# Three operations of the retention branch moved to later places in two engines' orders: the block transpose, the upper half and the remainder of the w_b product's input

## The reference

```python
h = rmsnorm(x, g_mix)
z = h @ w_in                                    # 1024 x 5888, nine parts
aq, ak, av, rq, rk, rv, rg, ga, gb = jnp.split(z, SPLIT_POINTS, axis=-1)
ya = sliding_window_sink_attention(aq, ak, av, sinks) @ w_a
r = chunkwise_retention(rq, rk, rv)             # 4 heads, 256 rows x 1024
r = r * lax.rsqrt(jnp.mean(r * r, axis=-1, keepdims=True) + EPS)
r = r.reshape(B, S, RET_V) * jax.nn.silu(rg.astype(jnp.float32))
yb = r.astype(x.dtype) @ w_b                    # its input is what the change moves
mixed = jax.nn.sigmoid(ga) * ya + jax.nn.sigmoid(gb) * yb
x = x + mixed @ w_out
```

## Time and profile before

| | us |
|---|---|
| median of 3 runs | 1009.88 (1009.08 to 1010.19) |
| the profiled execution's own time | 1010.19 |
| its span | 1008.4 |
| TensorE busy | 1000.7 (99%) |
| VectorE busy | 726.4 (72%) |
| ScalarE busy | 501.6 (50%) |
| mean granted TensorE clock | 0.999 |

### The profile page before, as it was taken

How to read it: one execution, slowest core, us unless ns; L and a number is a source line. 1 busy time by engine, 2 the same in 40 slices (tenths; PEclk the granted TensorE clock), 3 DMA queues, 4 the chain that set the end, 5 groups by cost and what they waited for, 6 DMA issues and landing times.

```text
span 1008.4 us, 13509 instructions
## 1 busy us (share of the span) xinstructions
PE 1000.7 (99%) x5621; PEld 846.4 (84%) x5621; DVE 726.4 (72%) x805; ACT 501.6 (50%) x610; POOL 170.6 (17%) x129
## 2 busy tenths in 40 slices
PE   9999999999999999999999999999999999999997
PEld 7888777888888888888877888888887899899796
DVE  5785785766566565785785767788877767789974
ACT  6544563454444545454564355344468555644352
POOL 0530000000000000430000020000000149169730
PEclk9999999999999999999999999999999999999999
DMA  9797564555655455596574567546544744355451
GB/s 336 238 300 255 180 196 167 174 185 183 205 173 207 167 179 176 188 296 232 180 231 152 165 169 266 188 170 213 202 167 139 247 168 168 125 168 148 115 188 42
DMA packets 106396, 192.80 MB, mean 191 GB/s; under 512 B 9352, under 2 KB 20704, under 8 KB 106208
## 3 DMA queue, kind: packets, MB, share of 16 engines
q1 hardware_dynamic: 106160, 191.85, 58.2%
q10 hardware_dynamic: 176, 0.09, 0.0%
HBM read 182.79 MB, written 6.82 MB: 188 GB/s over the span
## 4 chain that ended last, share of the span: by engine, by line
PE 98%; DMA 1%; DVE 0%; ACT 0%; SPq 0%; issue 0%; DVEq 0%; ACTq 0%
PE bank L816 13%; PE bank L819 12%; PE bank L818 12%; PE bank L1121 11%; PE bank L841 10%; PE bank L845 9%; PE bank L852 9%; PE bank L1125 6%; PE bank L1203 2%; PE bank L1430 1%; PE bank L998 1%; PE bank L1014 1%; PE bank L1417 1%; PE bank L843 1%; PE bank L850 1%; PE bank L1106 1%
## 5 line engine op out<-in xcount | busy, mean ns | idle before, releaser
L1911 DVE TENSOR_TENSOR w_lo<-arena,w_hi 128x2048 fp32r<-128x2048 f32 (+1 forms) x80 | 185.0, 2323 | 99.1 <-ACT w_hi L1518 98.8
L1911 DVE TENSOR_TENSOR w_lo<-raw,w_hi 128x2048 fp32r<-128x2048 f32 (+1 forms) x78 | 180.7, 2327 | 82.5 <-ACT w_hi L1518 82.4
L1518 ACT ACTIVATE w_hi<-raw 128x2048 fp32r<-128x2048 f32 (+1 forms) x83 | 157.1, 1893 | 106.4 <-PE bank L819 72.9
L1518 ACT ACTIVATE w_hi<-arena 128x2048 fp32r<-128x2048 f32 (+1 forms) x80 | 151.3, 1891 | 106.1 <-PE bank L819 82.3
L1121 PE MATMUL bank<-hT,w_hi 128*128 128x512 f32 x504 | 123.4, 391 | 0.0
L2539 POOL TENSOR_TENSOR rstd<-mean,const 128x1 f32<-128x1 f32 (+1 forms) x16 | 9.1, 578 | 633.8 <-DVE mean L1920 464.7
L1121 PEld LDWEIGHTS bank<-hT,w_hi 128*128 128x128 f32 x504 | 92.2, 188 | 17.5
L816 PE MATMUL bank<-w_hi,hT 128*128 128x512 f32 (+1 forms) x248 | 95.3, 384 | 0.0
L819 PE MATMUL bank<-w_hi,hT 128*128 128x512 f32 (+1 forms) x224 | 85.5, 382 | 0.0
L818 PE MATMUL bank<-w_lo,hT 128*128 128x512 f32 (+1 forms) x224 | 85.5, 382 | 0.0
L816 PE MATMUL bank<-w_hi,uT_hi 128*128 128x512 f32 x208 | 81.2, 390 | 0.0
(11 more groups left out here) (356 smaller groups left out, 1917.0 us busy)
## 6 DMA issues: line engine op xcount, KB each, us to landing
arena<-in_w_in SPq DMA_DIRECT2D x22, 1024.0 KB, 5.6
raw<-in_w_in SPq DMA_DIRECT2D x20, 1024.0 KB, 5.7
arena<-in_w_up SPq DMA_DIRECT2D x16, 1024.0 KB, 5.5
raw<-in_w_up SPq DMA_DIRECT2D x16, 1024.0 KB, 5.3
arena<-in_w_down SPq DMA_DIRECT2D x16, 1024.0 KB, 5.2
raw<-in_w_down SPq DMA_DIRECT2D x16, 1024.0 KB, 5.2
raw<-in_e_w_in SPq DMA_DIRECT2D x6, 1024.0 KB, 5.2
arena<-in_e_w_in SPq DMA_DIRECT2D x6, 1024.0 KB, 5.3
```

The lines of the kernel that those rows point to most:

```text
L1518: act.activation(w_hi[:, p % SPLIT_RING, :, 0:n], raw_at(p)[:, :, 0:n], copy).then_inc(hi_ready, 1)
L1911: dve.tensor_tensor(w_lo[:, s, :, 0:n], raw_at(p)[:, :, 0:n], w_hi[:, s, :, 0:n].bitcast(F32), ALU.subtract).then_inc(lo_ready, 1)
```

## The change

Three instructions change place, in each of the two layers:

- VectorE's block transpose into `r_rows` moves from the third softmax to the head of iteration 11, ahead of `w_lo` of piece 24.
- ScalarE's copy to `uT_hi` moves behind its share of window 10 (the exponentials of the fourth softmax), so that it stands ahead of `w_hi` of piece 25 and the evacuation of group 11.
- VectorE's subtraction to `uT_lo` moves from the fourth softmax to behind the loop over the groups: behind `w_lo` of piece 25 and ahead of its share of window 11.

```diff
@@ ScalarE
                 for g in range(W_IN_GROUPS):
                     if l or g:
                         step(p + 2 * g)
+                    window(l, g - 1)
                     if g == W_IN_GROUPS - 1:
                         act.wait_ge(r_turned, l + 1)
                         act.activation(uT_hi[:, :, :], r_rows, copy).then_inc(r_hi, 1)
-                    window(l, g - 1)
                     if g != RQ:
                         step(p + 2 * g + 1)
                     group_out(l, g)
@@ VectorE
-            def beside_exp(l, g):
-
-                if g == 7:
-                    retention_mean(l, 1)
-                if g == W_IN_GROUPS - 3:
-                    dve.wait_ge(h_blocks, 16 * BLOCKS * (l + 1))
-                    turn_blocks(r_rows, h_moved, KD).then_inc(r_turned, 1)
-                if g == W_IN_GROUPS - 2:
-                    dve.wait_ge(r_hi, l + 1)
-                    dve.tensor_tensor(uT_lo[:, :, :], r_rows, uT_hi[:, :, :].bitcast(F32), ALU.subtract).then_inc(r_lo, 1)
-
...
                 if SCORES_AT <= g < SCORES_AT + PAIRS:
-                    softmax(l, g - SCORES_AT, between=lambda: beside_exp(l, g))
+                    softmax(l, g - SCORES_AT, between=(lambda: retention_mean(l, 1)) if g == 7 else lambda: None)
...
                         turn_blocks(rT, r_moved, 2 * RET_HEADS).then_inc(rT_ready, 1)
+                    if g == W_IN_GROUPS - 1:
+                        dve.wait_ge(h_blocks, 16 * BLOCKS * (l + 1))
+                        turn_blocks(r_rows, h_moved, KD).then_inc(r_turned, 1)
                     if g != AKV and (l or g):
                         step(p + 2 * g)
...
+                dve.wait_ge(r_hi, l + 1)
+                dve.tensor_tensor(uT_lo[:, :, :], r_rows, uT_hi[:, :, :].bitcast(F32), ALU.subtract).then_inc(r_lo, 1)
                 window(l, W_IN_GROUPS - 1)
```

## The result

The changed kernel takes 1020.49 us (median of 4, 1019.94 to 1021.77) against 1009.62 us beside it (median of 4 runs of the kernel before): a ratio of 1.0107, 95% interval 1.0092 to 1.0124. It is 10.9 us slower, where 7.4 had been forecast as the likeliest and 1020.6 was the end of the range. Its profiled execution took 1020.46 us, with a span of 1018.7.

A forecast was written before the change was run, and what follows sets the result against it. TensorE was taken as the bound, busy 1000.7 of 1008.4 us. Two stalls of 3.65 us, 7.4 with wake-ups and nothing for the clock, added to the 1009.88 median gave 1017.3 us; range 1015.4 to 1020.6.

The forecast's parts named there:

- the stall: TensorE ahead of w_b's first matmul, waiting for uT_lo: 3.65 us a layer, 7.4 us for both with wake-ups.
- Hidden, with 0.3 us to spare: ScalarE's later evacuation of group 11 frees bank 0 at about 153.2, before TensorE wants it at 153.53.
- the price of the restart: Slower matmuls after each stall if the clock falls: between nothing and 2.9 us a fall, taken as nothing.
- the one gap of the trace that can be compared: Idle time after the kernel's last matmul: clock fell 3.9 us after the last work, against a forecast stall of 3.7.
- the case: Rival, clock falls too: restart at 1.2 GHz behind the stall, 1020.2 us for one layer, 1023.1 for both; chance 0.2.
- two falls: Clock falls behind the stalls of both layers: 1023.1 us, outside the range; chance 0.06.
- the signs named beforehand: Trace signs, against the prediction: another wait than uT_lo, layers differing by over a few tenths, third stall, matmuls spaced twice as far.
- It doesn't matter: Rival: idle room on VectorE and ScalarE absorbs the three moved operations, no change, 1009.9 us; chance 0.03.
- the serial chain: Maxima, exponentials, uT_hi, w_hi 25, w_lo 25, uT_lo in sequence: 10.3 us from 146.89, where TensorE gives 6.6.
- Faster: Rival: TensorE's attention window gains from softmaxes freed of foreign work, at the very best 1006.8 us; chance 0.02.
- third stall: Sign against the prediction: a further TensorE stall behind the two; later effects were forecast as hidden.

The follow-up runs named there:

- the run with uT_lo ahead: The changed kernel with the subtraction to uT_lo placed ahead of w_lo of piece 25 on VectorE: 1009.42 us against 1009.29, ratio 1.0006.

## Why the prediction held, and where it didn't

*The direction and the stall were right, link by link.* To compare instants, 1.35 us are added to the changed kernel's. w_lo 24 starts at 141.44 (forecast 141.44), sink_gap at 146.85 (146.89), w_hi 25 at 150.71 (150.75), w_lo 25 at 152.64 (152.69), uT_lo at 154.85 (154.90). The stalls are 3.71 and 3.69 us, where 3.65 and a wake-up were worked out. The run with 15 spare matmuls measures this term by itself: 7.43 us against 7.4.

*"Hidden, with 0.3 us to spare"* held for the bank of group 11: in the run with uT_lo ahead it could have become the next bound, and TensorE had no new wait in its trace.

*The step that failed* is the price of the restart: "I take nothing for the forecast, because the one gap of the trace that can be compared needed more time than this one has." The last matmul ended 3.9 us before the clock fell at the kernel's end, and I read those 3.9 us as the least idle time that brings a fall. They are no such threshold. The same ending in the changed kernel's own trace has the fall at about 1015.1, 2.2 us after the last matmul ended (its timeline row, then the slice of the clock):

```profile
1012.57 0.39 PE L819 MATMUL bank<-w_hi,uT_lo 128*128 128x512 f32 x1
1015.00:1016.00 1.00, 0.00 (x0) 0.00 (x0) 1.00 (x3) 0.00 (x0) 0.00 (x0) 0.57 0.01 2
```

Over the thirteen traces of this case the ending's idle time before the fall runs from 2.2 to 5.3 us, so the 3.9 of one row was one value out of a wide spread. In the middle of the kernel the clock fell behind gaps of 5.9 us both times, behind 3.6 us all three times that a profile shows, behind 3.2 us both times, and behind 1.9 us once in six, the shortest of them with a fall only after TensorE had worked again for 1.1 us. The term that was set to nothing measured 1.52 and 2.68 us in the profile and 3.5 us for both layers in the medians. Its upper bound of 2.9 us a fall, from the slow matmuls of the start, held: 2.68 is the largest seen. But the case had 0.2, and two falls, which is what the traces show, 0.06. The median lies 0.1 us inside the range, and that is luck: the range was drawn for one fall at its upper price, and two falls at lower prices came to nearly the same.

Of the signs named beforehand, two spoke against the prediction: the matmuls behind the wait were spaced 0.42 us, and the layers differ in their whole cost, 3.71 + 2.68 = 6.39 us against 3.69 + 1.52 = 5.21. Their stalls agree to 0.02, and TensorE waited for uT_lo alone.

The Trainium skill ("TensorE: Matmul & The Clock Gate", section "Why this matters for your kernels") warns of gaps of about this size. The traces agree with the warning and show it reaching down to 1.9 us, below the size that the section gives. I had set a single row of this case over the rule although the row was a single value, and of another situation: an end with no restart.

*The rivals.* "It doesn't matter" failed by the serial chain, as argued. "Faster" got nothing: with the same transpose moved alone the ratio is 1.0001. No third stall appeared behind the two.

## What to carry to other kernels

A filler may stand anywhere in a queue as long as it is not what the bound engine waits for next. When one is moved, write down the due time of its result and everything now ahead of it. Here three operations of 2 us each had been put in front of it, while the engine idled 2.2 us one place earlier. If the bound engine is TensorE, price a stall as its length and a fall of the clock on top (1.4 to 2.7 us here), and treat any gap of two microseconds or more as able to bring one: in this kernel 1.9 us did so at times, and 3.2 us and more in every trace. Where a wait can't be avoided, spare matmuls in the gap keep the clock, but size them by a measured spacing (0.225 us each here, 128x128 in float32), because too many become the bound.

## What the hardware showed that I hadn't expected

The clock can fall after TensorE has resumed. In the changed kernel's layer 1 it fell at 544.1, 0.9 us after the restart. It fell 1.2 us after it behind one of the gaps of 3.2 us, and 1.1 us after it behind a gap of 1.9 us. So the first matmuls behind a gap being spaced normally (0.23 us) doesn't mean that the clock was kept. In the other five of the eight falls that the traces show it came inside the gap, 1.9 to 3.0 us after the last matmul. The price of a fall varied from 1.37 to 2.68 us, with no order by the length of the gap: 1.37 and 1.78 behind 5.9 us of idle time, 1.56 behind 1.9.

And the record of the granted clock can't be relied on at the kernel's start. It gives 1.00 where 18 recorded matmuls of 128x128 took 0.23 us each. The 44 of the run with 22 spare ones took 5.18 us, 0.12 each, so the start ran at half that rate. (The 0.15 read from four of them in the prediction is too long, because it shares out the tail of the last over only four.)
